# DeltaNet in a hybrid decoder step: the 16x16 diagonal blocks of each tile's triangular inverse are solved on VectorE and carried there and back by DMA, and the work of neighbouring tiles is put in another order

## The chip, the core and the metric

The kernel runs on one core of a Trainium2 chip. The core has a matrix engine (TensorE, PE), a vector engine (VectorE, DVE), a scalar engine (ScalarE, ACT), a general engine (GpSimd, POOL) and SyncE (SP), which issues DMAs. They run side by side and wait for each other through semaphores. The time is that of the device for one launch, in microseconds (us), as the median of several runs; lower is better.

## The reference

One layer of a decoder that mixes tokens with a gated DeltaNet and a forgetting attention, and channels with a mixture of 64 experts. The change is in the DeltaNet of the prompt: 512 tokens, 8 heads of 64 dimensions, chunks of 64 tokens. Cut to it:

```
lmat = beta[..., :, None] * jnp.einsum('nbhik,nbhjk->nbhij', k, k) * dec_strict
rhs = beta[..., None] * jnp.concatenate([v, gam[..., None] * k], axis=-1)
sol = lax.linalg.triangular_solve(lmat, rhs, left_side=True, lower=True, unit_diagonal=True)
w1, w2 = sol[..., :dv], sol[..., dv:]
aqk = jnp.einsum('nbhik,nbhjk->nbhij', q, k) * dec_incl
...
def step(s, xs):
    u = w1c - jnp.einsum('bhck,bhkv->bhcv', w2c, s)
    o = jnp.einsum('bhck,bhkv->bhcv', qgc, s) + jnp.einsum('bhij,bhjv->bhiv', aqkc, u)
    s = glc[..., None, None] * s + jnp.einsum('bhck,bhcv->bhkv', kdc, u)
    return s, o
```

The triangular system is unit lower triangular, 64x64 for each chunk and head.

## The kernel before

The kernel is one program in phases, with a barrier of all engines between them; every wait and every order of instructions is written by hand. `arena` is all of SBUF, `bank` the eight PSUM banks. The phase here does the DeltaNet of the prompt in four tiles of 128 tokens (`t`, PT = 4), each of two chunks (`ch`), for 8 heads in two halves of four (`hb`). In one tile:

- Transposes (L1355) of keys, scaled keys, queries and scaled queries; the decay rows (L1360); the key and query products (L1364). ScalarE copies and takes the exponentials (L1534, L1537). VectorE makes from them `LT`, the masked and decayed key products, whose 64x64 blocks are to be inverted, and `dec` (L1479, L1485, L1486).
- The inverse by doubling, in six levels (`NL`): blocks of 1, 2, 4, 8, 16 and 32 are joined. Level 0 is a mask and a subtraction. In each later level a mask picks the off-diagonal blocks (`Lm`, L1468), TensorE multiplies twice (L1386 `Lm` by the transposed inverse, copied by ScalarE at L1554; L1396 by the inverse `Um`), VectorE subtracts (L1504) and TensorE transposes the new inverse (L1404, copied at L1557).
- The w products (L1410, L1411), and then the two chunks one after the other: state read (L1424), u on VectorE (L1512), output and state products (L1430 to L1432), new state (L1513, L1515). Then the output is copied and summed (L1518, L1519); the next tile's transposes wait for that.

Between these steps TensorE does parts of two other products of the layer that nothing here needs, the gate logits and the later modulation. They are the 80 later pieces (`PIECES`): "gate" pieces (L1194), "raw" pieces (L1189) and short "rows" pieces (L1180). `later_pieces(pe, place, count)` puts the next `count` of them at a place, and `later_out(act, place)` is ScalarE's copy of what they made. They read 2 MB slabs of weights into two slots. SyncE issues the loads of the slabs (`send_later(j)`, L220), each as soon as the last piece that read the same slot is done; its queue takes everything in order. Of the 80 pieces, 12 are in the phase before.

GpSimd runs the recurrence of the sample tokens at the same time (L1604 to L1636), four passes over 128x2048 elements, all in SBUF: L1618, six sums at L1614, three small operations, L1623, L1624, L1625, L1626, six sums. Because of it the kernel keeps some of VectorE's second operands in PSUM (`by_psum`, and the masks in banks 4 and 5).

Of the kernel before, what the change touches and what calls it, by code (L numbers as in the profile page):

```python
# [107 lines left out]
def build(nc, A, O):  # L108
# [39 lines left out]
    def const(*dims, p=P):  # L148
        nonlocal c
        v = at(c, *dims, p=p)  # L150
        c += int(np.prod(dims))
        return v
    ident, causneg, cumU, ones = const(P), const(P), const(P), const(P)
    chunk1, chunkU, decneg = const(P), const(P), const(P)
    strictL, strictU = const(P), const(P)
    lvl = const(6, P)
# [10 lines left out]
    nF = const(TOK, p=H)  # L167
    cT, w24 = const(KD, QUAD), const(KD, 24)
    nm, rsum, rinv = const(PT * H), const(PT * H), const(PT * H)
    lfp = const(DB * NPG, H)  # L170
# [91 lines left out]
    with nc.Block() as block:  # L262
        @block.gpsimd
        def _(pool):
# [26 lines left out]
            for l in range(6):  # L291
                b = 2 << l
                n = P // b
                fill(lvl[:, l, :].rearrange("p (n r) -> p n r", n=n), (1.0, 0.0), (ge, 0, 1, [[-b, n], [0, b]]),
                     (ge, b // 2 - 1, -1, [[b, n], [0, b]]), (ge, -(b // 2), 0, [[0, n], [1, b]]))
# [940 lines left out]
    with nc.Block() as block:  # L1236
# [77 lines left out]
    trT = at(X0 + 9472, 4, CW, P)  # L1314

    rows_of = [at(T1 + 6912, 4, W), at(T1 + 9472, 4, W)]
    kd_of = [at(T2, W), at(T1 + 8960, W)]
    LT, dec, Lm0, Tm, Um, P1 = (at(T2 + 512 + 1024 * i, H, P) for i in range(6))
    Lm_of = [Lm0, at(X0 + 4096, H, P)]
# [7 lines left out]
    r_done, tr_mm, tr_sb, kk_mm, gr_mm, dec_sub, dec_exp, lt_done = (Tick(nc, n) for n in (  # L1327
        "scaled_rows", "gdn_T_in_psum", "gdn_T_copied", "kk_product", "decay_rows", "decay_diffs", "decay_matrix", "LT_done"))
    lm_done, p1_mm, p1_sb, q_mm, u_sb, t_mm, t_sb = (Tick(nc, n) for n in (
        "level_masked", "LT_product", "LT_product_copied", "TLT_product", "inverse_updated", "inverse_T", "inverse_T_copied"))  # L1330
# [3 lines left out]
    t_act, masks_in = Tick(nc, "later_inverse_T_copied"), Tick(nc, "level_masks_in_psum")  # L1334
    S_kept, ro = at(T1 + 4096, CW, HD), at(T1 + 12216, NT, H)
    CONTENDED, mask0_in = 2, Tick(nc, "first_mask_in_psum")
    by_psum = bank[5][:, P:P + 3 * H].rearrange("p (i h) -> p i h", h=H)
    NL = 6
    KK_BANK = (2, 3, 4, 5)

    with nc.Block() as block:
        @block.tensor
        def _(pe):
            for t in range(PT):
                rows4, kd = rows_of[t % 2], kd_of[t % 2]
                nw2T = rows4[:, 1].rearrange("p (c n) -> p c n", c=CW)

                later_pieces(pe, (t, "state before"), 1)
                pe.wait_ge(r_done.sem, 3 * t + 2)
                if t:  # L1350
                    pe.wait_ge(o_sb.sem, t)
                srcs = [qkv_tm[:, t, W:2 * W], rows4[:, 0], qkv_tm[:, t, 0:W], rows4[:, 1]]
                for i, s in enumerate(srcs):
                    for cc in range(CW):
                        mm = nc.tensor.transpose(bank[i][:, cc * P:(cc + 1) * P], s[:, cc * P:(cc + 1) * P], ident)  # L1355
# [3 lines left out]
                for h in range(H):  # L1359
                    nc.tensor.matmul(bank[h // 4][:, (h % 4) * P:(h % 4 + 1) * P], E8[:, h, :], GT[:, t * P:(t + 1) * P], start=True, stop=True)  # L1360
                pe.wait_ge(tr_sb.sem, 4 * t + 4)
                for h in range(H):
                    r = slice(HD * (h % 2), HD * (h % 2) + HD)
# [3 lines left out]
                later_pieces(pe, (t, "decay"), 3)  # L1367
                later_pieces(pe, (t, "masks"), 2)
                for l in range(NL):
                    Lm = Lm_of[l % 2]  # L1370
                    for hb in range(2):
                        n = 2 * (NL * t + l) + hb
                        heads = range(4 * hb, 4 * hb + 4)
                        pe.wait_ge(lm_done.sem, n + 1)
                        col = lambda h: slice((h % 4) * P, (h % 4 + 1) * P)
                        if l == 0:
                            for h in heads:
                                mm = nc.tensor.transpose(bank[hb][:, col(h)], Lm[:, h, :], ident)
                            p1_mm.inc(mm)
                        else:  # L1380
                            if l == 1:
                                pe.wait_ge(t_sb.sem, 2 * t + hb + 1)
                            else:
                                pe.wait_ge(t_act.sem, 2 * ((NL - 2) * t + l - 2) + hb + 1)
                            for h in heads:
                                mm = nc.tensor.matmul(bank[hb][:, col(h)], Lm[:, h, :], Tm[:, h, :], start=True, stop=True)  # L1386
                            p1_mm.inc(mm)
                    if l == 0:
                        later_pieces(pe, (t, 0), 1)
                        continue  # L1390
                    for hb in range(2):
                        heads = range(4 * hb, 4 * hb + 4)
                        k = 2 * ((NL - 1) * t + l - 1) + hb
                        pe.wait_ge(p1_sb.sem, k + 1)
                        for h in heads:
                            mm = nc.tensor.matmul(bank[2 + hb][:, col(h)], P1[:, h, :], Um[:, h, :], start=True, stop=True)  # L1396
                        q_mm.inc(mm)
                    later_pieces(pe, (t, l), 1)
                    if l < NL - 1:
                        for hb in range(2):  # L1400
                            heads = range(4 * hb, 4 * hb + 4)
                            pe.wait_ge(u_sb.sem, 2 * (NL * t + l) + hb + 1)
                            for h in heads:
                                mm = nc.tensor.transpose(bank[hb][:, col(h)], Um[:, h, :], ident)  # L1404
                            t_mm.inc(mm)
# [1438 lines left out]
```

## Time and profile before

| | |
|---|---|
| median of 3 runs | 1685.38 us (1684.54 to 1686.4) |
| the profiled execution | 1679.23 us, its span 1677.1 us |
| mean granted TensorE clock | 0.961 of full speed |
| busy | TensorE 92%, VectorE 36%, ScalarE 19%, GpSimd 19% |
| the DeltaNet phase | from 476 to 781 us |

The profiled execution is one run of the program on the chip. Times in its views are from the start of the span. Busy time is the sum of the instructions of an engine; matmuls overlap, so a row that merges several says from when to when they ran. "[3.15 <-PE bank L1396]" behind a row is the idle time of its engine ahead of it and what ended it.

### The profile page before, as it was taken

What the parts mean: (1) busy time and instruction counts of PE and PEld (TensorE: products, weight loads), DVE (VectorE), ACT (ScalarE), POOL (GpSimd) and SP (SyncE); (2) the same over time, 40 slices, a digit from 0 to 9 for tenths busy, and PEclk for the clock granted to TensorE, in tenths of its full rate; (3) what the DMA queues carried; (4) which work ended last, traced back from release to release, by engine and by line L of the source; (5) the groups of instructions that cost most, each with busy time, mean ns of one, the idle gap of its engine ahead of it and who ended that gap; (6) DMA issues with size and microseconds to landing.
All of it is one profiled execution on the core that took longest, in us unless ns stands there. A gap on an engine that the chain in (4) does not pass through costs nothing. (4 is left out here: it accounts for less than half of the span.)

```text
span 1677.1 us, 21451 instructions
## 1 busy us (share of the span) xinstructions
PE 1537.2 (92%) x8238; PEld 898.8 (54%) x8238; DVE 610.4 (36%) x1261; ACT 320.8 (19%) x704; POOL 313.8 (19%) x341
## 2 busy tenths in 40 slices
PE   5999999999989899999999688999989989898966
PEld 3876666664568787777755433343334433333322
DVE  2002543342374536354558743331111111111128
ACT  1002222333232223231201200111101111111121
POOL 6000000000039994000001421111111111111100
PEclk8999999999999999999999888999999999999978
DMA  9312110123162126114740157999999999999765
GB/s 340 120 51 84 52 52 0 51 63 101 64 182 100 68 71 187 68 57 145 264 158 26 42 203 314 388 415 411 415 421 391 413 412 403 408 378 422 285 253 241
DMA packets 104481, 357.16 MB, mean 213 GB/s; under 512 B 27731, under 2 KB 28883, under 8 KB 78259
## 3 DMA queue, kind: packets, MB, share of 16 engines
q1 hardware_dynamic: 79414, 302.11, 46.5%
q0 software_dynamic: 15520, 39.17, 6.2%
q10 hardware_dynamic: 9446, 14.51, 2.4%
q8 instruction: 66, 1.08, 0.3%
q14 instruction: 35, 0.29, 0.1%
HBM read 330.70 MB, written 37.62 MB: 220 GB/s over the span
## 5 line engine op out<-in xcount | busy, mean ns | idle before, releaser
L1985 PE MATMUL bank<-arena 128*32 128x512 f32 (+2 forms) x1536 | 334.0, 611 | 23.8 <-DMA arena<-in_w_up 22.9
L1985 PEld LDWEIGHTS bank<-arena 128*32 128x32 f32 (+2 forms) x1536 | 119.9, 138 | 205.6 <-issue 202.9
L1993 PE MATMUL bank<-arena 128*32 128x512 f32 (+2 forms) x768 | 168.6, 598 | 0.7 <-DVE arena L2740 0.7
L1972 POOL DMA_INDIRECT expert_rows<-arena x46 | 46.5, 1010 | 486.2 <-PE bank L1978 419.7
L2734 DVE TENSOR_TENSOR arena<-arena,bank 128x256 f32<-128x256 f32 x46 | 19.4, 421 | 323.7 <-ACT arena L2388 323.7
L1194 PE MATMUL bank<-arena 128*128 128x272 f32 x512 | 128.0, 398 | 1.2 <-ACT arena L1231 1.0
L429 PE MATMUL bank<-arena 128*128 128x272 f32 x480 | 113.9, 400 | 2.8 <-PEq L132 1.8
L1993 PEld LDWEIGHTS bank<-arena 128*32 128x32 f32 (+2 forms) x768 | 55.0, 134 | 110.3 <-issue 109.4
L1194 PEld LDWEIGHTS bank<-arena 128*128 128x128 f32 x512 | 93.3, 190 | 22.8 <-issue 2.9
L429 PEld LDWEIGHTS bank<-arena 128*128 128x128 f32 x480 | 93.0, 194 | 23.3 <-issue 2.7
L658 PE MATMUL bank<-arena 128*128 128x272 f32 x384 | 103.6, 416 | 0.0
L446 PE MATMUL bank<-arena 128*128 128x512 f32 (+3 forms) x304 | 88.1, 449 | 2.6 <-ACT arena L2330 2.2
L2388 ACT ACTIVATE arena<-bank 128x256 f32<-128x256 f32 x46 | 17.6, 383 | 347.4 <-PE bank L1985 347.4
L658 PEld LDWEIGHTS bank<-arena 128*128 128x128 f32 x384 | 73.8, 202 | 17.2 <-issue 3.4
L2746 DVE COPY arena<-bank 128x512 f32<-128x512 f32 x46 | 31.8, 691 | 126.9 <-PE bank L1993 126.9
L446 PEld LDWEIGHTS bank<-arena 128*128 128x128 f32 (+1 forms) x304 | 46.9, 193 | 42.5 <-issue 38.7
L1600 POOL TENSOR_TENSOR arena<-arena 128x512 f32<-128x512 f32 x5 | 7.7, 1535 | 314.8 <-POOLq L1236 314.5
L2450 POOL DMA_INDIRECT expert_lists<-arena x34 | 35.1, 1032 | 140.5 <-DVE arena L2576 131.3
L1978 PE MATMUL bank<-arena 128*128 128x128 f32 x368 | 49.5, 279 | 7.6 <-DMA arena<-h_rows,arena 7.6
L2394 ACT COPY arena<-bank 128x512 f32<-128x512 f32 x46 | 27.0, 587 | 152.5 <-PE bank L1993 152.5
L1968 POOL DMA_INDIRECT arena<-h_rows,arena x46 | 47.2, 1027 | 39.7 <-DVE arena L1912 20.0
L1504 DVE TENSOR_TENSOR arena<-arena,bank 128x512 f32<-128x512 f32 x40 | 27.5, 687 | 67.2 <-PE bank L1396 66.9
(468 smaller groups left out, 2108.5 us busy)
## 6 DMA issues: line engine op xcount, KB each, us to landing
arena<-in_w_gate SPq DMA_DIRECT2D x64, 1024.0 KB
arena<-in_w_up SPq DMA_DIRECT2D x64, 1024.0 KB
arena<-in_w_down SPq DMA_DIRECT2D x64, 1024.0 KB, 17.6
arena<-in_w_ada SPq DMA_DIRECT2D x12, 2048.0 KB, 8.8
arena<-in_w_in SPq DMA_DIRECT2D x11, 2048.0 KB, 9.9
arena<-expert_rows SPq DMA_DIRECT2D x8, 2048.0 KB, 25.6
gate_logits<-arena ACTq DMA_DIRECT2D x16, 272.0 KB, 3.8
arena<-gate_logits SPq DMA_DIRECT2D x8, 544.0 KB, 5.1
```

The source lines that it names most:

```text
L429: mm = nc.tensor.matmul(pair[i][:, 0:HALF], w[:, k, m * P:(m + 1) * P], rhs[:, k, i * HALF:(i + 1) * HALF], start=k == 0, stop=k == kt - 1)
L446: mm = nc.tensor.matmul(out, lhs[:, k, t * P:t * P + n], w[:, k, cols], start=k == 0, stop=k == kt - 1)
L658: mm = nc.tensor.matmul(out[:, 0:HALF], w[:, k, (m % 4) * P:(m % 4 + 1) * P], hT[:, k, half * HALF:(half + 1) * HALF], start=k == 0, stop= ...
L1194: mm = nc.tensor.matmul(out[:, 0:HALF], w[:, k, m * P:(m + 1) * P], hT[:, k, half * HALF:(half + 1) * HALF], start=k == 0, stop=k == KD - 1)
L1504: done(u_sb, nc.vector.tensor_tensor(Um[:, hs, :], Um[:, hs, :], bank[2 + hb].ap().rearrange("p (h n) -> p h n", h=4), ALU.subtract))
L1968: return nc.gpsimd.indirect_dma_start(out=into, out_offset=None, in_=h2_d, in_offset=bass.IndirectOffsetOnAxis(ap=rows, axis=0), bounds_ch ...
L1972: return nc.gpsimd.indirect_dma_start(out=y_d, out_offset=bass.IndirectOffsetOnAxis(ap=rows, axis=0), in_=of, in_offset=None, bounds_check ...
L1978: mm = nc.tensor.transpose(bank[half][:, k * P:(k + 1) * P], of[:, kk * P:(kk + 1) * P], ident)
L1985: mm = nc.tensor.matmul(out[rows].rearrange("p (a n) -> p a n", a=2), x[:, k, rows], gate_up_slot(n)[:, :, k, :], start=k == 0, stop=k == ...
L1993: mm = nc.tensor.matmul(out[rows, :], h[:, k, rows], down_slot(n)[:, k, 512 * half:512 * half + 512], start=k == 0, stop=k == 1)
L2450: scat.inc(nc.gpsimd.indirect_dma_start(out=list_rows, out_offset=bass.IndirectOffsetOnAxis(ap=adi[:, t, k:k + 1], axis=0), in_=tokval[:, ...
L2746: nc.vector.tensor_copy(Yb[u % RY][:, 512:D], bank[6][:, :]).then_inc(y_v.sem, 1)
```

## The change

- VectorE no longer masks and subtracts at levels 0 to 3. For each tile SyncE stores the eight 16x16 diagonal blocks of `LT` per head to DRAM (`key_blocks`) in 8 transfers of 16 partitions, and loads them back with 2 transfers of 64 partitions so that a partition holds one block of one head (`n16`, on two halves of the partitions). VectorE inverts each block there by 15 steps of two operations (`block_inverses`, each half of the partitions eight of the sixteen columns). SyncE stores the result in 2 transfers, waits for it, and puts it on the diagonal of `Um` in 8 transfers of 16 partitions.
- Only the levels that join blocks of 16 and of 32 are left on TensorE (`NL` = 2). ScalarE copies their off-diagonal blocks out of `LT` in 6 copies; `Lm` is zeroed once, `Um` once a tile. No masks are made or kept.
- The order of a tile: levels, then the transposes, decay and key products of the next tile (`keys_and_decays(t + 1)`), then the w products and both chunks of this tile, then the next tile's `block_inverses` on VectorE. `dec` and the scaled queries get a second buffer each, so that both tiles can be under way.
- The later pieces move: 15 behind the first tile's key products and 2 ahead of its levels, then 4 ahead of each tile's levels, 4 behind each tile's key products, and 5 or 6 at the other places.

The core of the diff:

```diff
@@ VectorE
-            def level_mask(t, l):
...
+            def block_inverses(t):
+
+                dve.wait_ge(n16_in.sem, 32 * (t + 1))
+                for j in range(15):
+                    n = 15 - j
+                    row = (i16 if j == 0 else x16)[:, :, j:j + 1].to_broadcast([P, 8, n])
+                    step(nc.vector.tensor_tensor(p16[:, :, 0:n], row, n16[:, j:j + 1, j + 1:16].to_broadcast([P, 8, n]), ALU.mult))
+                    ins = nc.vector.tensor_tensor(x16[:, :, j + 1:16], (i16 if j == 0 else x16)[:, :, j + 1:16], p16[:, :, 0:n], ALU.subtract)
+                    done(x16_done, ins) if j == 14 else step(ins)
...
+                inverse_level(t, 1)
+                if t + 1 < PT:
+                    keys_and_decays(t + 1)
                 dve.wait_ge(w_mm.sem, t + 1)
...
+                states(t, 0)
+                if t + 1 < PT:
+                    step(nc.vector.memset(Um, 0.0))
+                states(t, 1)
...
                 if t < PT - 1:
+                    block_inverses(t + 1)
@@ TensorE
+            def levels(t):
+                later_pieces(pe, (t, "inverse back"), 4 if t else 2)
+                pe.wait_ge(um_in.sem, 16 * NB * (t + 1))
+                if t:
+                    pe.wait_ge(o_sb.sem, t)
...
+            later_pieces(pe, "state before", 2)
+            keys_and_decays(0)
+            for t in range(PT):
+                levels(t)
+                if t + 1 < PT:
+                    keys_and_decays(t + 1)
+                weighted_rows(t)
+                states(t, 0)
+                later_pieces(pe, (t, "state between"), 1 if t + 1 < PT else 2)
+                states(t, 1)
@@ ScalarE
+                for b in range(4):
+                    rows, cols = slice(32 * b, 32 * b + 16), slice(32 * b + 16, 32 * b + 32)
+                    ach.inc(nc.scalar.copy(Lm_of[0][rows, :, cols], LT[rows, :, cols]))
@@ SyncE
-            for j in range(3, len(LATER)):
-                send_later(j)
+            def store_key_blocks(t):
+                sp.wait_ge(lt_done.sem, t + 1)
+                for a in range(NB):
+                    b16 = slice(16 * a, 16 * a + 16)
+                    n16_out.inc(sp.dma_start(n16_d[a].rearrange("h j i -> j h i"), LT[b16, :, b16]), 16)
+
+            def load_key_blocks(t):
+                sp.wait_ge(n16_out.sem, 16 * NB * (t + 1))
+                for g in range(2):
+                    n16_in.inc(sp.dma_start(n16[64 * g:64 * g + 64], n16_d.rearrange("a h j i -> (a h) j i")), 16)
+
+            def move_block_inverses(t):
+                sp.wait_ge(x16_done.sem, t + 1)
+                for g in range(2):
+                    x16_out.inc(sp.dma_start(x16_d[:, :, g].rearrange("a h r i -> (a h) r i"), x16[64 * g:64 * g + 64]), 16)
+                sp.wait_ge(x16_out.sem, 32 * (t + 1))
+                for a in range(NB):
+                    b16 = slice(16 * a, 16 * a + 16)
+                    um_in.inc(sp.dma_start(Um[b16, :, b16], x16_d[a].rearrange("h g r i -> (g r) h i")), 16)
+
+            send_later(3)
+            store_key_blocks(0)
+            send_later(4)
+            load_key_blocks(0)
+            send_later(5)
+            move_block_inverses(0)
+            send_later(6)
+            store_key_blocks(1)
```

SyncE before the change, behind the loads for the sample recurrence: the nine slabs (in_w_in and in_w_ada) and then the new state.

```order
L1581 DMA arena<-sample_gates 64x8
L220 DMA arena<-in_w_in 128x8x512
L220 DMA arena<-in_w_ada 128x8x512 x2
L220 DMA arena<-in_w_in 128x8x512
L220 DMA arena<-in_w_ada 128x8x512 x2
L220 DMA arena<-in_w_in 128x8x512
L220 DMA arena<-in_w_ada 128x8x512 x2
L1592 DMA out_ssm_prompt<-arena 64x4x64 x2
```

SyncE of the change at the same place, up to the second tile's stores (the slabs are L223 there).

```order
L223 DMA arena<-in_w_in 128x8x512
L1645 DMA key_blocks<-arena 16x8x16 x8
L223 DMA arena<-in_w_ada 128x8x512
L1650 DMA arena<-key_blocks 64x256 x2
L223 DMA arena<-in_w_ada 128x8x512
L1655 DMA key_block_inverses<-arena 64x128 x2
L1659 DMA arena<-key_block_inverses 16x8x16 x8
L223 DMA arena<-in_w_in 128x8x512
L1645 DMA key_blocks<-arena 16x8x16 x8
L1650 DMA arena<-key_blocks 64x256 x2
```

Slabs and block transfers take turns in one queue now: the first slab stands ahead of the first tile's stores, the second ahead of its loads, the third ahead of its inverses.

TensorE before the change, from the first tile's key products (L1364) into its third level (L1194, L1189 and L1180 are the later pieces).

```order
L1364 MATMUL bank<-arena 128x256 x8
L1194 MATMUL bank<-arena 128x272 x12
L1180 MATMUL bank<-arena 32x128 x4
L1194 MATMUL bank<-arena 128x272 x4
L1378 MATMUL bank<-arena 128x128 x8
L1194 MATMUL bank<-arena 128x272 x4
L1386 MATMUL bank<-arena 128x128 x8
L1396 MATMUL bank<-arena 128x128 x8
L1194 MATMUL bank<-arena 128x272 x4
L1404 MATMUL bank<-arena 128x128 x8
L1386 MATMUL bank<-arena 128x128 x8
L1396 MATMUL bank<-arena 128x128 x8
```

TensorE of the change from the same key products (L1372) to the last pieces ahead of the levels; L1192, L1187 and L1178 are the later pieces, L1384 is the transpose of the loaded inverse blocks.

```order
L1372 MATMUL bank<-arena 128x256 x8
L1192 MATMUL bank<-arena 128x272 x8
L1178 MATMUL bank<-arena 32x128 x4
L1192 MATMUL bank<-arena 128x272 x24
L1187 MATMUL bank<-arena 32x512 x8
L1192 MATMUL bank<-arena 128x272 x16
L1178 MATMUL bank<-arena 32x128 x4
L1192 MATMUL bank<-arena 128x272 x8
L1384 MATMUL bank<-arena 128x128 x8
L1392 MATMUL bank<-arena 128x128 x8
L1397 MATMUL bank<-arena 128x128 x8
```

Seventeen pieces now stand between the first tile's key products and its first level, where six did.

## Rows read from the trace of the kernel before

**Rows 1.** Windows, whole phase: stretch, its length, then busy (instructions) by engine, clock, DMA.
```profile
476.00:781.00 305.00, 286.43 (x2250) 233.24 (x2250) 143.77 (x219) 80.44 (x184) 151.71 (x102) 0.99 0.29 94
```

**Rows 2.** Timeline of TensorE, one level of the second tile: start, length, instruction.
```profile
592.92 2.02 PE L1386 MATMUL bank<-arena 128*128 128x128 f32 x16 [0.33 <-ACT arena L1557]
594.78 2.00 PE L1396 MATMUL bank<-arena 128*128 128x128 f32 x16
...
598.45 1.04 PE L1404 MATMUL bank<-arena 128*128 128x128 f32 x8
599.82 2.02 PE L1386 MATMUL bank<-arena 128*128 128x128 f32 x16 [0.33 <-ACT arena L1557]
```

**Rows 3.** Timeline of TensorE, other steps of a tile, and the last.
```profile
535.11 0.43 PE L1410 MATMUL bank<-arena 128*128 128x64 f32 x2
...
540.93 2.10 PE L1194 MATMUL bank<-arena 128*128 128x272 f32 x8
...
554.30 0.43 PE L1180 MATMUL bank<-arena 128*32 128x128 f32 x8
556.68 1.94 PE L1355 MATMUL bank<-arena 128*128 128x128 f32 x16 [1.96 <-DVE arena L1519]
...
562.36 2.00 PE L1364 MATMUL bank<-arena 64*128 64x256 f32 x16
...
778.44 2.27 PE L452 MATMUL bank<-arena 128*128 128x128 f32 x18
```

**Rows 4.** Timeline of VectorE, first tile, first and last operation of the decay.
```profile
487.30 1.43 DVE L1479 TENSOR_TENSOR bank<-bank,arena 128x512 f32<-128x512 f32 x2 [2.84 <-PE bank L1364]
...
493.52 0.42 DVE L1486 TENSOR_TENSOR arena<-bank,arena 128x256 f32<-128x256 f32 x1
```

**Rows 5.** Groups by form, VectorE, whole span: busy us, mean ns, idle before.
```profile
L2553 DVE TENSOR_TENSOR arena<-arena 128x8 f32<-128x8 f32 x5 | 0.9, 172 | 0.2
...
L251 DVE TENSOR_TENSOR arena<-arena 128x128 f32<-128x128 f32 x2 | 0.6, 293 | 0.1
```

**Rows 6.** SyncE's timeline, and DMA issues 470 to 800: KB each, us to landing.
```profile
476.12 8.30 SPq L1573 DMA_DIRECT2D sample_rows<-arena  x24
...
later_modulation<-arena ACTq DMA_DIRECT2D x32, 16.0 KB, 1.7
...
arena<-in_x_sample SPq DMA_DIRECT2D x1, 128.0 KB, 14.0
...
arena<-sample_gates SPq DMA_DIRECT2D x2, 2.0 KB, 2.9
```

**Rows 7.** Timelines of VectorE and of GpSimd, both inputs in SBUF.
```profile
476.23 8.23 DVE L1453 TENSOR_TENSOR arena<-arena 128x512 f32<-128x512 f32 x5
...
498.31 3.60 DVE L1499 TENSOR_TENSOR arena<-arena 128x512 f32<-128x512 f32 x1
...
551.37 0.42 DVE L1513 TENSOR_TENSOR arena<-arena 128x256 f32<-128x256 f32 x1
...
497.73 3.64 POOL L1618 TENSOR_TENSOR arena<-arena 128x2048 f32<-128x2048 f32 x1
...
546.88 5.49 POOL L1624 TENSOR_SCALAR arena<-arena 128x2048 f32<-128x2048 f32 x1
```

**Rows 8.** The first slab of the phase on SyncE, and such slabs' landing.
```profile
493.44 0.59 SPq L220 DMA_DIRECT2D arena<-in_w_in  x1
...
arena<-in_w_in SPq DMA_DIRECT2D x3, 2048.0 KB, 8.8
```

**Rows 9.** Timeline of GpSimd, parts of the first pass, and the last sums.
```profile
518.17 4.54 POOL L1625 TENSOR_TENSOR arena<-arena 128x2048 f32<-128x2048 f32 x1
...
526.50 5.77 POOL L1614 TENSOR_TENSOR arena<-arena 128x1024 f32<-128x1024 f32 x6
...
630.32 6.16 POOL L1614 TENSOR_TENSOR arena<-arena 128x1024 f32<-128x1024 f32 x6
```

**Rows 10.** Windows, the start of the next phase.
```profile
798.00:805.00 7.00, 6.46 (x15) 4.94 (x16) 0.00 (x0) 1.34 (x2) 2.74 (x16) 0.53 0.97 317
```

More of the change, by code:

```diff
@@ L1366, in _ @@
                 kk_mm.inc(mm)
-                later_pieces(pe, (t, "decay"), 3)
-                later_pieces(pe, (t, "masks"), 2)
+                later_pieces(pe, (t, "decay"), 15 if t == 0 else 4)
+            def levels(t):
[3 more added lines that the diff above has]
+                    pe.wait_ge(o_sb.sem, t)
+                for hb in range(2):
+                    for h in range(4 * hb, 4 * hb + 4):
+                        mm = nc.tensor.transpose(bank[hb][:, col(h)], Um[:, h, :], ident)
+                    t_mm.inc(mm)
@@ L1369, in _ @@
                 for l in range(NL):
-                    Lm = Lm_of[l % 2]
+                    k = 2 * (NL * t + l)
+                    pe.wait_ge(lm_done.sem, t + 1)
                     for hb in range(2):
[L1372 to L1387, printed above, removed]
@@ new lines, in take_P1 @@
+            def take_P1(t, l):
+                k = 2 * (NL * t + l)
+                for hb in range(2):
+                    act.wait_ge(p1_mm.sem, k + hb + 1)
+                    p1_sb.inc(nc.scalar.copy(P1[:, 4 * hb:4 * hb + 4, :], bank[hb].ap().rearrange("p (h n) -> p h n", h=4)))
+            later_out(act, "state before")
+            keys_and_decays(0)
+            for t in range(PT):
+                if 0 < t < PT - 1:
+                    act.wait_ge(o_sb.sem, t)
+                    scales_to_psum(t + 1)
+                later_out(act, (t, "inverse back"))
+                take_T(t, 0)
+                take_P1(t, 0)
+                later_out(act, (t, "level"))
+                take_T(t, 1)
+                take_P1(t, 1)
+                if t + 1 < PT:
+                    keys_and_decays(t + 1)
@@ L1561, in _ @@
                 w2_sb.inc(nc.scalar.mul(nw2T, bank[5].ap().rearrange("p (c n) -> p c n", c=CW), -1.0))
[L1562 to L1565 removed]
+                for place in ((t, "w"), (t, "state", 0), (t, "state between"), (t, "state", 1)):
+                    later_out(act, place)
             for tick in (mod_out, *gate_out):
@@ L1596, in _ @@
             step = chained(pool, gch)
+            for g in range(2):
+                half = i16[64 * g:64 * g + 64]
+                step(pool.memset(half, 0.0))
+                i16_made.inc(pool.affine_select(out=half, in_=half, compare_op=ALU.not_equal, fill=1.0, base=8 * g,
+                                                pattern=[[1, 8], [-1, 16]], channel_multiplier=0))
+            pool.wait_ge(i16_made.sem, 2)
             for t in range(NT):
```

281 lines of the change are left out of this document (149 added, 132 removed).

## The prediction

> **What bounds the kernel now.** The page of the profile gives TensorE 92% of the span, so I read where it is not busy, and what the DeltaNet stage holds. The stretch from 476 to 781 us is that stage: 305 us, of which TensorE is busy 286.43 [rows 1]. Little of it is waiting, so the stage costs what its matmuls cost. One level of the inverse takes from 592.92 to 599.82, 6.90 us: two products of 2.02 and 2.00, a later piece of 2, a transpose of 1.04 [rows 2]. The rest of a tile: the transposes, a piece, the decay rows and the key products from 556.68 to 564.36; the w products from 535.11 to 540.93; both chunks with their pieces from 540.93 to 554.30 [rows 3].
>
> **What goes away.** Of the 15 blocks of eight matmuls that a tile's inverse has on TensorE (5 transposes, 10 products) the order keeps 6 (2 transposes, 4 products). That is 3 x 1.04 + 6 x 2.01 = 15.2 us a tile, 61 us in all [rows 2]. The 80 later pieces stay, only at other places. So 61 us is the most that can be won, and it is won only where TensorE finds something else than a wait.
>
> **A tile after the change.** Levels: a transpose first, then 6.90, then the two products of the last level without a piece or transpose, and about 0.6 for the copies between: 12.5 us. Next tile's keys: 7.7 plus four pieces at about 2.0: 15.8, which covers the 6.3 us that VectorE and ScalarE need for the decay (from the matmuls' end at 487.2 to 493.5 plus 0.4) [rows 4]. The w products 5.8, the chunks 13.4 [rows 3]. In sum 47.5 for tiles 0 to 2. The last has no next keys and one piece of 0.4 more: 32.1. All four: 174.6.
>
> **The new chain.** Before its levels can start a tile needs: VectorE's 30 small operations, two stores, a wait for them, eight loads.
> - VectorE alone: 8 values a partition take 172 ns and 128 take 293 [rows 5], so about 160 ns plus 1.04 ns a value. Thirty operations over 8n values (n from 15 to 1, twice each: 1,920 values) are 4.8 + 2.0, and 30 gaps of 0.04: 8.0 us.
> - The way back through DRAM: SyncE issued 24 small transfers of 4 partitions in 8.30 us, 0.35 each; these have 16, and I choose 0.5. Small stores landed in 1.7, small loads in 2.9 [rows 6]. Two stores to their landing 2.3; seven issues of loads 3.5; the last load with its semaphore 3.0: about 9 us. Bounds: 0.35 an issue, with landings of 1.3 and 2.2, 6.6; twice my issues and twice the landing of the loads, 15.
> - VectorE's own end of a tile (state, two copies, sum), after which the transposes could start at 556.68, 2.3 behind the last product [rows 3].
> Four pieces lie beside it on TensorE, 7.3 us. Without anything else a tile waits 2.3 + 8.0 + 9.0 - 7.3 = 12 us.
>
> **GpSimd in the way.** The sample recurrence runs on GpSimd from 497.7 to 636.5 [rows 7, 9]. Where both inputs of a VectorE operation are in SBUF it is held until the GpSimd operation ends, and then the two alternate: five operations of 512 values took 8.23 us, 1.65 each, and one at 498.31 took 3.60 although it needs 0.69; it ended with L1618, which ran from 497.73 for 3.64 [rows 7]. All 30 new operations have both inputs in SBUF. One exception shows: at 551.37 such an operation took its plain 0.42 while the TENSOR_SCALAR of L1624 ran from 546.88 to 552.37 [rows 7]. The Trainium skill, page "SBUF — State Buffer", section "Who interferes with whom", says that a VectorE instruction with two SBUF inputs contends with a GpSimd instruction that reads SBUF, under an exclusive lock. The trace agrees for tensor-tensor operations and not for L1624, which reads SBUF too. I go by the rows: L1624 is a free window of 5.45 us in each pass of some 34 us.
>
> Tile 0. Key products end at 488, their blocks are masked 6.8 later, 494.7. The eight stores queue behind the gate slab that SyncE issued at 493.44, which takes 8.8 to land: 502.2; a 128 KB load behind two slabs took 14.0 to land, so a queue keeps its order [rows 6, 8]. SyncE then issues the next slab as soon as piece 19 is done, about 501.4, and the loads of the key blocks queue behind it: 510.5. VectorE waits for L1623 until 512.7; in L1624's window some 20 operations fit (5.8 us); the last ten wait for L1625 from 518.17 (4.54), L1626 (as L1618, 3.64), six operations of 5.77, and L1618 [rows 7, 9]. They end at 536. With 9 to move them the levels begin at 545. TensorE meanwhile has 17 pieces, 29 us: it ends them at 524 (it waits for the slab too) and then stands for 21.
> Tile 1. The levels of tile 0 end the chunks at 545 + 47.5 = 592.5, VectorE is free at 595. The six sums at 526.50 come again two passes later, at 596 [rows 9]: these (5.8), L1618 (3.7), six more (5.8), three small ones (1.2) and L1623 (3.7) hold seventeen operations, the other thirteen take 2.7 in L1624's window: 23 us instead of 8, and the tile waits 27 instead of 12.
> Tiles 2 and 3 come after 640, when GpSimd is done: 12 each.
>
> **The clock.** After sparse work the granted clock fell to 1.2 GHz: from 798 to 805 it was 0.53 although TensorE was busy 6.46 of 7 us, then 1.00 again [rows 10]. Each of the four waits is longer than the pauses ahead of that. Per wait (1 - 0.53) x 7 = 3.3 us, 13.2 in all. Low end nothing.
>
> **The sum.** 69 to the first levels (476 to 545) + 174.6 + (2.3 + 23 + 9) + 2 x (2.3 + 8 + 9) + a tail of 2.6 from the last product, at 778.4 before [rows 3] + 13.2 = 332.3 us, against 305: 27.3 slower. The profiled execution took 1679.23, so 1706.5 in its terms; the median of the runs is 6.15 above it: **1712 us**. Its own range is 1697 to 1727: 11 either way for where VectorE meets L1624, 10 for the transfers, added as independent.
>
> Costed at nothing: the masks that GpSimd no longer makes at the kernel's start, where TensorE waits for weights; three memsets in VectorE before the late scaled rows, beside TensorE's first pieces and transposes (else 3); ScalarE's six block copies: the copies of the later pieces queue behind them, so TensorE's fourth piece of tile 0 waits, but inside its wait for the slab (else 5). SyncE's slabs are behind the block transfers; from the sums each lands 5 us or more before its piece. If one did not, it is up to 8.8.
>
> **Rivals.**
> - *Faster: the small operations are not held.* They are 0.17 to 0.29 us, and might slip between GpSimd's operations; the held rows were all of 256 to 512 values. Then tile 0 starts at 527.5 and tile 1 waits 12: 332.3 - 17.5 - 15 = 299.8, 5 faster; with the cheap transfers (6.6) 15 faster: 1670 to 1680. It decides as soon as the holds cost less than 5 us together. Against it: five operations of one engine and five of the other took strict turns at 476, which needs an order and no size [rows 7]. Chance 0.24.
> - *The same.* Both blocks meet L1624 at its start, with 12 each: 13 and 11 less, 3 slower: 1688. Chance 0.09.
> - *L1624 holds them too*, as the rule of the Trainium skill on the page named above has it. Worked from rows: 30 operations against 30 of GpSimd's are a pass and a half, 54 us for tile 0 (31 more); tile 1 then meets GpSimd's last 13 us (6 less): 1738. Chance 0.07.
> - *The transfers cost 15 a tile*: 24 more, 1736. Chance 0.06.
> The forecast has the other 0.54.
>
> **Numbers.** 0.2%, 3.4 us, is about what a measurement of this kernel can tell from no change. Faster 0.25, same 0.07, slower 0.68. The range leaves out the two dear rivals (0.13) and the edge of the fast one in which the clock holds too (0.05): 1669 to 1728.
>
> **What would show it.** TensorE's busy time in the stage down by 61 us plus what a lower clock adds; L1493 and L1494 with means of 0.2 us in tiles 2 and 3 and 0.7 to 1 in tiles 0 and 1; TensorE waiting for the loaded inverse blocks about 20, 27, 12 and 12 us; the stage ending near 808. The forecast is wrong if tile 0's small operations take 8 us, if the loads land in half the time, or if the clock stays at 2.4 GHz in the waits.

## The result, and the profile after

Nine runs of each kernel gave a median of 1692.54 us (1689.45 to 1695.86) after the change and 1684.54 us (1670.84 to 1688.30) before it: ratio 1.0052, 95% interval 1.0028 to 1.0076. The change costs 8 us, where 27 were forecast; 1692.54 lies below the forecast's own range (1697 to 1727) and inside the wide one (1669 to 1728).

The profiled execution of the changed kernel took 1695.86. Windows of its trace: the DeltaNet stage, which answers to [rows 1], and two of TensorE's waits; columns as there.
```profile
478.56:806.99 328.43, 228.54 (x1771) 182.80 (x1771) 156.86 (x259) 63.35 (x157) 150.81 (x106) 0.85 0.30 91
528.00:556.00 28.00, 0.59 (x3) 0.16 (x1) 21.36 (x24) 0.39 (x1) 26.43 (x20) 0.55 0.03 5
609.00:648.00 39.00, 0.80 (x5) 0.51 (x4) 28.47 (x32) 0.00 (x0) 31.98 (x23) 0.55 0.20 37
```
TensorE does 58 us less in the stage than in [rows 1], at a granted clock of 0.85 for 0.99, and the stage is still 23 us longer than that one. Where the time went, in TensorE's waits (us, times, longest):
```profile
PE bank L1384 <- DMA arena<-key_block_inverses: 86.3, 4, 38.2
```
That is 86.3 us in four waits, the longest 38.2. Three of them in the timeline:
```profile
556.09 0.69 PE L1384 MATMUL bank<-arena 128*128 128x128 f32 x2 [27.50 <-DMA arena<-key_block_inverses]
647.49 1.97 PE L1384 MATMUL bank<-arena 128*128 128x128 f32 x8 [38.20 <-DMA arena<-key_block_inverses]
710.43 1.97 PE L1384 MATMUL bank<-arena 128*128 128x128 f32 x8 [10.60 <-DMA arena<-key_block_inverses]
712.31 3.36 PE L1392 MATMUL bank<-arena 128*128 128x128 f32 x16
```
The fourth wait is 9.98. They were forecast at 21, 27, 12 and 12. The last row, behind a wait, is the same work as the 2.02 us of [rows 2]; it takes 3.36, at a granted clock of 0.50 from 711 to 715 (1.2 of 2.4 GHz).

What they wait for is in VectorE's groups, the two lines of the new solve in tile 0 (window 514.9 to 548.7) and in tile 2 (695.2 to 703.1); columns are count, then busy us and the mean of one in ns:
```profile
L1493 DVE TENSOR_TENSOR arena<-arena 128x120 f32<-128x120 f32 (+14 forms) x15 | 17.4, 1158 | 18.2 <-DMA arena<-key_blocks 17.7
L1494 DVE TENSOR_TENSOR arena<-arena 128x120 f32<-128x120 f32 (+14 forms) x15 | 15.3, 1019 | 0.5
...
L1493 DVE TENSOR_TENSOR arena<-arena 128x120 f32<-128x120 f32 (+14 forms) x15 | 3.4, 226 | 0.5
L1494 DVE TENSOR_TENSOR arena<-arena 128x120 f32<-128x120 f32 (+14 forms) x15 | 3.4, 225 | 0.5
```
The same 30 operations take 33.6 us in tile 0 (515.05 to 548.70) and 31.5 in tile 1 (603.74 to 635.23), while GpSimd runs its recurrence, and 7.8 in tiles 2 and 3. The timeline of VectorE at the start of tile 0's solve, and below it that of GpSimd (POOL), show how:
```profile
515.05 3.13 DVE L1493 TENSOR_TENSOR arena<-arena 128x120 f32<-128x120 f32 x1 [17.74 <-DMA arena<-key_blocks]
518.22 0.28 DVE L1494 TENSOR_TENSOR arena<-arena 128x120 f32<-128x120 f32 x1
...
519.76 0.26 DVE L1493 TENSOR_TENSOR arena<-arena 128x96 f32<-128x96 f32 x1
520.06 4.45 DVE L1494 TENSOR_TENSOR arena<-arena 128x96 f32<-128x96 f32 x1
524.54 3.67 DVE L1493 TENSOR_TENSOR arena<-arena 128x88 f32<-128x88 f32 x1
528.25 2.38 DVE L1494 TENSOR_TENSOR arena<-arena 128x88 f32<-128x88 f32 x1
```
```profile
514.34 5.44 POOL L1723 TENSOR_SCALAR arena<-arena 128x2048 f32<-128x2048 f32 x1
519.87 4.53 POOL L1724 TENSOR_TENSOR arena<-arena 128x2048 f32<-128x2048 f32 x1
524.47 3.64 POOL L1725 TENSOR_TENSOR arena<-arena 128x2048 f32<-128x2048 f32 x1
528.19 5.73 POOL L1713 TENSOR_TENSOR arena<-arena 128x1024 f32<-128x1024 f32 x6
```
Read the ends: 520.06 + 4.45 is 524.51, just behind the end of L1724 (524.40) and the start of the next GpSimd operation (524.47); 524.54 + 3.67 is 528.21, just behind the start of the one after it (528.19). Where GpSimd's operations follow each other without a pause, one small operation gets in behind each of them, whatever its size. L1723, of which the prediction made a free window of 5.45 us (it is L1624 of before), is free only at its end: the operation at 515.05 is done at 518.18, 3.84 us into it, and then six go through at 0.26 to 0.28.

### The profile page after: what moved, and what is told of

It reads as the page before. It is cut to its first block and busy times, and to the rows that moved or that the text cites. A ratio compares the mean times of both kernels' runs of the same rounds, so it can differ in the third digit from the quotient of the medians.

```text
span 1694.1 us, 20463 instructions
## 1 busy us (share of the span) xinstructions
PE 1479.2 (87%) x7758; PEld 847.2 (50%) x7758; DVE 622.5 (37%) x1300; ACT 303.6 (18%) x676; POOL 301.7 (18%) x321
## 5 line engine op out<-in xcount | busy, mean ns | idle before, releaser
L1192 PE MATMUL bank<-arena 128*128 128x272 f32 x512 | 128.9, 403 | 7.1 <-ACT arena L1229 6.9
L1192 PEld LDWEIGHTS bank<-arena 128*128 128x128 f32 x512 | 95.2, 192 | 33.8 <-ACT arena L1229 8.4
L1384 PE MATMUL bank<-arena 128*128 128x128 f32 x32 | 7.9, 427 | 86.3 <-DMA arena<-key_block_inverses 86.3
L2077 PE MATMUL bank<-arena 128*128 128x128 f32 x368 | 49.5, 279 | 7.2 <-DMA arena<-h_rows,arena 7.2
L1493 DVE TENSOR_TENSOR arena<-arena 128x120 f32<-128x120 f32 (+14 forms) x60 | 48.5, 809 | 19.8 <-DMA arena<-key_blocks 17.7
L2067 POOL DMA_INDIRECT arena<-h_rows,arena x46 | 47.3, 1027 | 39.7 <-DVE arena L2011 20.2
```

Source lines behind the costliest of these rows:

```text
L1192: mm = nc.tensor.matmul(out[:, 0:HALF], w[:, k, m * P:(m + 1) * P], hT[:, k, half * HALF:(half + 1) * HALF], start=k == 0, stop=k == KD - 1)
L1493: step(nc.vector.tensor_tensor(p16[:, :, 0:n], row, n16[:, j:j + 1, j + 1:16].to_broadcast([P, 8, n]), ALU.mult))
L2067: return nc.gpsimd.indirect_dma_start(out=into, out_offset=None, in_=h2_d, in_offset=bass.IndirectOffsetOnAxis(ap=rows, axis=0), bounds_ch ...
L2077: mm = nc.tensor.transpose(bank[half][:, k * P:(k + 1) * P], of[:, kk * P:(kk + 1) * P], ident)
```

## The experiments

In this section the stage is measured from the start of its first transposes to the start of the first transposes behind it, which all kernels have (309.1 us in the first profile of before, 331.9 in that of after). Times are medians in us; ratios are to the kernel before in the same rounds, with 95% intervals. Medians of different rows come from different rounds and are not compared with each other.

| kernel | stage | solves, tiles 0 and 1 | median | ratio |
|---|---|---|---|---|
| before (six profiles) | 309.1, 319.5, 321.7, 321.6, 322.0, 321.7 | | | |
| before against itself | 321.7 | | 1694.29 | 0.9995 (0.9963 to 1.0027) |
| after (three profiles) | 331.9, 331.9, 331.1 | 33, 32 | 1702.34 | 1.0057 (1.0035 to 1.0079) |
| after, operands in PSUM | 285.7 | 7.8, 7.7 | 1658.28 | 0.9810 (0.9758 to 0.9863) |
| after, products alone in PSUM | 308.1 | 26.5, 19.3 | 1679.26 | 0.9926 (0.9899 to 0.9952) |
| after, no recurrence | 285.4 | 7.8, 7.8 | 1658.40 | 0.9832 (0.9780 to 0.9884) |
| before, no recurrence | 307.7 | | 1679.34 | 0.9927 (0.9901 to 0.9954) |
| after, kept warm | 321.0 | 31.7, 29.8 | 1699.52 | 1.004 (1.001 to 1.007) |
| PSUM, kept warm | 283.2 | 7.8, 7.8 | 1651.32 | 0.978 (0.9747 to 0.9813) |
| the same, branch weights later | 276.8 | 7.7, 7.7 | 1647.34 | 0.9738 (0.9705 to 0.9771) |
| PSUM, stage lengthened | 321.1 | 7.7, 7.7 | 1693.97 | 0.9988 (0.9951 to 1.0024) |

### The operands of the solve in PSUM

```diff
+    n16_ps = bank[2][:, 0:256].rearrange("p (j i) -> p j i", j=16)
+    p16_ps = bank[3][:, 0:128].rearrange("p (r i) -> p r i", r=8)
...
+                step(nc.vector.tensor_copy(n16_ps, n16))
...
-                    step(nc.vector.tensor_tensor(p16[:, :, 0:n], row, n16[:, j:j + 1, j + 1:16].to_broadcast([P, 8, n]), ALU.mult))
-                    ins = nc.vector.tensor_tensor(x16[:, :, j + 1:16], (i16 if j == 0 else x16)[:, :, j + 1:16], p16[:, :, 0:n], ALU.subtract)
+                    step(nc.vector.tensor_tensor(p16_ps[:, :, 0:n], row, n16_ps[:, j:j + 1, j + 1:16].to_broadcast([P, 8, n]), ALU.mult))
+                    ins = nc.vector.tensor_tensor(x16[:, :, j + 1:16], (i16 if j == 0 else x16)[:, :, j + 1:16], p16_ps[:, :, 0:n], ALU.subtract)
```


> The changed kernel with the solve's factors copied to a PSUM bank (one more VectorE copy a tile) and its products written to PSUM, so that no small VectorE operation has two SBUF sources. Theory H (in tiles 0 and 1 the solve is stretched from 7.8 to 33.6 and 31.5 us because GpSimd's recurrence holds VectorE's operations of two SBUF sources): each solve takes 8 to 10 us, the waits for the loaded inverses fall to about 5, 15, 11 and 10 us, the stage to about 280 us and the time to 1640 to 1655, below both kernels. Theory D (the moves by DMA and the queue set the waits): the solve may shrink but the levels start no earlier, time 1685 to 1695. Theory Q (any VectorE operation is slow while GpSimd runs): solve stays above 25 us, no change of time.

The time fell as theory H had it, to 1658.28, though not quite to 1655. The copy of the factors takes 0.43 us a tile. The solve's multiplications in this kernel's trace, least, median and longest in ns:
```profile
L1496 DVE TENSOR_TENSOR bank<-arena,bank x60: 173/229/288, 515.3 to 715.5; 128x120 f32<-128x120 f32 x4, 128x112 f32<-128x112 f32 x4, 128x104 f32<-128x104 f32 x4, 128x96 f32<-128x96 f32 x4
```
Its TensorE's waits:
```profile
PE bank L1386 <- DMA arena<-key_block_inverses: 39.7, 4, 17.2
```
And the longest, in tile 2, in its timeline:
```profile
661.51 1.97 PE L1386 MATMUL bank<-arena 128*128 128x128 f32 x8 [17.23 <-DMA arena<-key_block_inverses]
```
None of the 60 is longer than 0.288 us (none of the 60 subtractions than 0.279), beside the same GpSimd operations. The solves of tiles 0 and 1 together are 50 us shorter and the stage 46. This version beats both kernels. The 17.2 us in tile 2 was not foreseen; the section on a load that met the third move is about it.

### Without the recurrence, after and before

```diff
-            for t in range(DS):
-                kt, qt = sx[:, t, 1, :], sx[:, t, 0, :]
...
-                sum_keys(so[:, t, :])
+            step(pool.memset(so, 0.0))
```


> The changed kernel without GpSimd's recurrence over the sample tokens (their output rows are filled with zeros instead), VectorE's operations as they are. Theory H: solves of tiles 0 and 1 take 8 us each, the first two waits fall by 25 and 23 us (less where another operand is late), the stage to about 280 us, time 1640 to 1655, the same as with the operands in PSUM. Theory D: waits and time stay within 5 us of the changed kernel.

> The kernel before without GpSimd's recurrence over the sample tokens (their output rows are filled with zeros). It is the fourth corner beside before, after, and after without the recurrence: it says what the change is worth where nothing holds VectorE. In the profiles of before the stage took 309.1 and 319.5 us from its first transpose to the first transpose behind it, with granted clocks of 0.99 and 0.97. Theory: before has only large VectorE operations in the contended tiles and most of their sources are PSUM banks, so it loses little to GpSimd: 0 to 10 us gained, time ratio to before 0.994 to 1.0, and the change alone would be worth 25 to 37 us. Rival: before loses as much as after does in those tiles (over 25 us gained), and then the hold explains the level of both kernels but not the difference.

These two kernels leave the recurrence out, so their sample outputs are not those of the layer; they are there for the times. Taking GpSimd's work away gives the changed kernel the same solves of 7.8 us as the operands in PSUM did. So the solve is slow because of GpSimd, and because of operands that both lie in SBUF. That the two stages agree as well (285.4 and 285.7) is in part chance. Without the recurrence GpSimd's stores and its 2 MB load are issued from 497 to 518 us; there the first solve begins 38.6 us after the stage's start (34.8 with the operands in PSUM), and the first move back takes 11.0 us. With the operands in PSUM it is the third move that is long, 13.6.

The kernel before gains 0.7% (12 us) without the recurrence, a little above what was expected. With nothing to hold VectorE the change makes the kernel faster, 0.9832 against 0.9927, some 16 us (give or take 10), less than the 25 to 37 that were expected. The holds cost the changed kernel 37 us (1.0052 less 0.9832, of 1684.5; give or take 10) and the one before 12: they turn the sign.

### The products alone in PSUM

The edit is that of the first experiment without the copy: the subtractions then read one operand in SBUF, the multiplications still two.

> The changed kernel with only the solve's products in PSUM: the 15 subtractions of a tile then have one SBUF source, the 15 multiplications still two. Theory H2 (an operation is held if it has two SBUF sources, and one gets in behind each of GpSimd's): the held operations halve, the solves of tiles 0 and 1 take 16 to 20 us in place of 33.6 and 31.5, the subtractions keep 170 to 290 ns, the time lies about half way, at a ratio of 0.99 to before. Rival H1 (an operation is held by any SBUF source, and PSUM for all of them is needed): solves stay at 30 us or more, ratio 1.005.

The subtractions (L1495) and the multiplications (L1494) in this trace, four tiles each:
```profile
L1495 DVE TENSOR_TENSOR arena<-arena,bank x60: 168/220/280, 510.8 to 732.9; 128x120 f32<-128x120 f32 x4, 128x112 f32<-128x112 f32 x4, 128x104 f32<-128x104 f32 x4, 128x96 f32<-128x96 f32 x4
...
L1494 DVE TENSOR_TENSOR bank<-arena x60: 174/266/4161, 508.6 to 732.7; 128x120 f32<-128x120 f32 x4, 128x112 f32<-128x112 f32 x4, 128x104 f32<-128x104 f32 x4, 128x96 f32<-128x96 f32 x4
```
With one source in SBUF no operation is held, with two up to 4.16 us: H2's condition holds. Its size does not quite: tile 0 took 26.5 us, not 16 to 20, of which the 15 multiplications are some 22; tile 1 took 19.3. The time came out half way, 0.9926. Rival H1, that one SBUF source is enough to be held, is refuted. The Trainium skill, page "SBUF — State Buffer", section "Who interferes with whom", says that a VectorE instruction with at most one SBUF input, outside its 2-port modes, which tensor-tensor operations do not have, does not contend with GpSimd, and one with two does where GpSimd reads SBUF. These two rows agree with it. The Trainium skill, same page, section "Summary: rules for kernel authors", says that of two such instructions the second to issue is blocked until the first finishes. GpSimd's TENSOR_TENSOR rows agree with that; L1723 does not, beside which a held operation was done after 3.84 of its 5.44 us.

### The clock in the waits

`keep_warm` gives TensorE products of the identity that nobody reads; they stand ahead of its wait for the loaded inverses.

```diff
+                if t:
+                    pe.wait_ge(o_sb.sem, t)
+                keep_warm(bank[0][:, 384:512], (110, 150, 38, 38)[t])
                 pe.wait_ge(um_in.sem, 16 * NB * (t + 1))
```


> The changed kernel with products of the identity that nobody reads (110, 150, 38, 38) put into TensorE's four waits for the loaded inverses. Theory C (the clock that falls during a wait costs 2.5 to 3 us at each of them behind it): granted clock of the stage up from 0.85 to 0.97 or more, stage and time 8 to 12 us shorter, ratio to before 0.998 to 1.001. Rival: the time follows the VectorE chain and the clock costs nothing there: within 3 us of the changed kernel, ratio 1.004 to 1.006.

> The changed kernel with all of the solve's extra operands in PSUM, and 6, 58, 36 and 36 idle products of the identity in what is left of the waits. Theory C: 6 to 10 us less than with the operands in PSUM alone, ratio to before 0.975 to 0.978. Rival: the same as with the operands alone, 0.981.

Windows from 478 to 803, first of the changed kernel:
```profile
478.00:803.00 325.00, 225.04 (x1726) 179.54 (x1727) 154.90 (x254) 63.60 (x157) 150.81 (x106) 0.85 0.30 91
```
and of the one kept warm:
```profile
478.00:803.00 325.00, 305.26 (x2468) 259.30 (x2468) 162.69 (x268) 65.44 (x160) 148.99 (x102) 0.98 0.33 102
```
The granted clock stayed up and the stage lost 10.9 us. Not all of this is the clock: the two held solves were 3.6 us shorter, having met GpSimd otherwise, tile 1's move back took 9.1 us in place of 12.3, and the first solve began 2.1 later. The clock is read from what TensorE does behind the four waits, from the first product of the levels to the next solve, or to the stage's end. Together these stretches took 184.2, 183.3 and 183.9 us in the three profiles of the changed kernel and 183.9 with the operands in PSUM, against 177.8 and 178.7 in the two kernels kept warm: 6.0 and 5.2 us less, 1.3 to 1.5 a wait.

The time shows less than that: 1.004 against 1.0052 and 1.0057, with intervals that overlap. On top of the PSUM operands the stage lost only 2.5 us, because in tile 1 the idle products outlasted the loads: the levels began 10.1 us behind the solve, where they began 7.5 behind it without them. The ratio went from 0.981 to 0.978, again within the intervals. So the clock's price is shown in the stage and not in the time.

### A load that met the third move

```diff
+            pool.wait_ge(um_in.sem, 16 * NB * 3)
             branch_in[1].inc(pool.dma_start(wbb, A["w_branch_b"][0].rearrange("(k p) n -> p k n", p=P)), 16)
```


> The kernel with operands in PSUM and warm waits, with GpSimd's load of the branch weights (2 MB) held back until the third tile's inverses are in. Theory W (the move back of that tile took 13.4 us instead of 7.4 because its loads shared the DMA engines with the branch weights and the slab): the third move takes 7.5 to 8.5, the stage 5 to 6 us less than 283.2, ratio about 0.975. Rival: the move stays at 13 us (something else slows it), no difference; or the weights then come late behind the stage and cost more than 5 us there.

The move back in tile 2, from the first store's issue to the levels, in the timeline without the edit:
```profile
644.98 1.10 SPq L1661 DMA_DIRECT2D key_block_inverses<-arena  x2
649.29 0.82 POOL L1744 DMA_DIRECT2D arena<-in_w_branch_b  x1
658.44 0.90 PE L1389 MATMUL bank<-arena 128*128 128x128 f32 x3 [9.08 <-DMA arena<-key_block_inverses]
```
and with it:
```profile
644.66 1.10 SPq L1661 DMA_DIRECT2D key_block_inverses<-arena  x2
652.12 1.09 PE L1389 MATMUL bank<-arena 128*128 128x128 f32 x8 [3.08 <-DMA arena<-key_block_inverses]
652.66 0.81 POOL L1745 DMA_DIRECT2D arena<-in_w_branch_b  x1 [2.41 <-DMA arena<-key_block_inverses]
```
The move took 7.5 us in place of 13.5 and the stage 6.4 less: theory W. Behind the stage the profiled execution was 2.0 us longer. This version has the lowest ratio of all, 0.9738, but its interval overlaps that of 0.978 without the edit: the gain of this one step is shown in the stage and not in the time.

The changed kernel has the same trouble in tile 1, where its move took 12.3 us (solve ended 635.23, levels 647.49) against 7.4 in the other tiles. GpSimd's stores of the sample states, issued at 638.01 and 640.47, lie in it; its window 640 to 643:
```profile
640.00:643.00 3.00, 0.00 (x0) 0.00 (x0) 0.00 (x0) 0.00 (x0) 2.77 (x3) 0.50 0.87 148
```
and its transfers issued from 630 to 650 (KB, us to landing):
```profile
out_ssm_sample<-arena POOLq DMA_DIRECT2D x2, 512.0 KB, 9.4
```
That these stores are the cause there was not tried by itself, but the other runs bear it out. In the two repeats of the changed kernel the stores are issued 2.8 us behind the solve's end, as here, and the move took 11.9 and 11.6 us. In the kernel kept warm they come 6.6 behind it: 9.1. In the kernels with the operands or the products in PSUM, and in the one without the recurrence, no store falls into tile 1's move: 7.4 to 7.5.

### Both kernels again, and a longer stage

> The kernel before, unchanged, profiled a second time. Its time is 1684.5 by the median. In the first profile the DeltaNet stage took 305.3 us and what came behind it 895.9 us, with stretches of low granted clock between 882 and 1013 us. If the 8.8 us that the rest of the program was longer there than in the profile of after are a chance of that one execution, the rest varies here (887 to 896 us) while the stage keeps 305 within 1 us. If the change really gives time back behind the stage, the rest is 896 here again.

> The changed kernel, unchanged, profiled a second time. The first profile had 328.4 us of stage and 887.1 us behind it. If the stage's loss is fixed by dependences, it is 328 again within 2 us, with the four waits for the loaded inverses at 27, 38, 11 and 10 us. If the gap between the loss in the stage (23 us) and the loss in the medians (8 us) is chance in one profile, stage or rest move here by several us; if the rest gives it back, it is 887 again.

> The kernel before against itself, on the chip and in the rounds of the others: ratio 1.000 within 0.3%. Its profile is the third of the stage: near 309 us as in the first, or near 319 as in the second, with a granted clock in the contended tiles to match. If the first was a fast exception, this one has 314 us or more.

> The changed kernel, unchanged, against before in the same rounds. The first comparison gave 1.0052 (1.0028 to 1.0076), 8 us; 1.003 to 1.008 is expected again, a stage of 332 us within 1, waits of 27, 38, 11 and 10 us. If the difference of the medians were to reach the 23 us of the first two profiles, the ratio would be 1.013.

Before against itself came out at 0.9995 and the change at 1.0057, as the first time. The stage of the changed kernel is the same in three profiles within 0.8 us. That of the kernel before was 309.1 in the profile that the prediction used and 319.5 and 321.7 in the next two, so I took three more.

> The kernel before, a fourth profile. If the stage of 309.1 us in the first profile was an exception, it has 316 us or more here, with held L1499 operations of 2 to 3.5 us in the second tile; if the stage has two levels that change from execution to execution, 309 or 320.

> The kernel before, a fifth profile, with the same question: 309 or 320 us of stage. If the time of an execution follows its stage, executions under 1685 have 309 and those over 1690 have 320.

> The kernel before, a sixth profile, with the same question: 309 or 320 us of stage.

321.6, 322.0 and 321.7, in executions of 1684.9, 1688.3 and 1687.7 us: the first profile was the exception, by 10 to 13 us. The timeline of the fourth shows two places where its 12.5 us go. By the second tile's transposes it is 2.9 us behind the first profile (80.1 us from the stage's start, 77.2 in the first), and 1.6 of these are there when the first tile's last state update (L1513, both inputs in SBUF) begins. In the first profile this is the operation at 551.37 of [rows 7], with its plain 0.42. In the fourth it began behind the start of L1625 and was held to its end:
```profile
552.19 4.33 DVE L1513 TENSOR_TENSOR arena<-arena 128x256 f32<-128x256 f32 x1
```
```profile
551.73 4.51 POOL L1625 TENSOR_TENSOR arena<-arena 128x2048 f32<-128x2048 f32 x1
```
It took 4.29 to 4.35 in all five later profiles. TensorE then waited 3.2 us for the transposes (1.96 in the first), and the granted clock from 560 to 565 was 0.53, where the first profile has 1.00; by its key products the fourth is 5.8 us behind. The other 6.7 come between its first level and its w products, with the second tile's sums of the identity and a masked block (L1499, both inputs in SBUF). In the first profile:
```profile
574.03 0.90 DVE L1499 TENSOR_TENSOR arena<-arena 128x512 f32<-128x512 f32 x1
575.69 0.91 DVE L1499 TENSOR_TENSOR arena<-arena 128x512 f32<-128x512 f32 x1
```
and in the fourth:
```profile
579.04 2.25 DVE L1499 TENSOR_TENSOR arena<-arena 128x512 f32<-128x512 f32 x1
582.05 3.37 DVE L1499 TENSOR_TENSOR arena<-arena 128x512 f32<-128x512 f32 x1
585.45 0.69 DVE L1501 TENSOR_TENSOR arena<-arena,bank 128x512 f32<-128x512 f32 x1
586.29 2.05 PE L1386 MATMUL bank<-arena 128*128 128x128 f32 x8 [2.99 <-DVE arena L1501]
```
In the first they fell beside the last, short sums of GpSimd's L1614. In the fourth they met L1623 and L1624, TensorE waited for them, and its granted clock over the 77 us from 555.7 was 0.89, where the first profile has 0.98 from 556.5 on. Without the recurrence L1513 takes 0.42 and L1499 0.69, and the stage of before 307.7. So in five of six profiles the kernel before pays some 12 us for held operations and the clock behind them, and the profile before the prediction was of the one that did not. Why the first tile was 1.6 us faster in that one stays open; its granted clock from 500 to 510 was 1.00, where the five have 0.83.

The rest of the program went the other way. A stretch of routing (from L2073 to L1978 of before) took 130.6 us in the first profile of before and 138.0, 138.2, 124.7, 124.9 and 124.7 in the others, and 125.4, 138.1 and 130.9 in those of after: three levels, whichever the kernel. In the first two profiles that took 5 us off the difference of 23 in the stage; their spans were 17 us apart, the medians 8.

> The changed kernel with the solve's operands in PSUM (ratio 0.981 to before, stage 285.7 us) and 160 more identity products behind the last chunk, which lengthen the DeltaNet stage by about 20 us at a full clock and touch nothing else. Theory P (what the stage takes is passed on in full): time and span 18 to 21 us above the version without them, ratio 0.992 to 0.993, and then the 6 us by which the rest was shorter in the profiles of after than of before are chance. Rival G (part is given back, since weights go on loading meanwhile): the rest of the program gets 3 to 8 us shorter, ratio 0.987 to 0.990.

I had taken the 160 products at about half of what they take: nine are 2.27 us in the last row of [rows 3], 0.25 each, and the stage grew by 35.4 us, 0.22 each. The ratio rose by 0.0178 (30 us, give or take 11), the profiled span by 39.7. So most of what the stage takes, if not all, is passed on; that 3 to 8 us come back is neither shown nor excluded.

## Why the prediction was off

The direction and the mechanism were right: VectorE's small operations held by GpSimd in tiles 0 and 1, TensorE waiting in each tile for the blocks, TensorE's busy time down by 58 us, where 61 less what a lower clock adds were forecast. The size was off by 19 us, and the step that failed is the last of **The sum**, "= 332.3 us, against 305: 27.3 slower": not the 332 but the 305. The stage of after, by the same bounds, came out at 328.4. The 305 was read in an execution in which three operations of the kernel before that GpSimd holds elsewhere fell into gaps; in the other five its stage is 10 to 13 us longer. The prediction had seen that this execution was 6.15 us below the median, and added these to the result as if they lay outside the stage. 27.3 less the 3.9 of the sum and less 12.5 for the base (the median of the six, 321.6, less 309.1) is 10.9 us, where the two timed comparisons have 8 and 9.6 (0.0057 of 1692). That the first profile's stage was short was neither in the bounds nor among the rivals, since every duration came from that one execution. The same chance gave the prediction its free window: the operation at 551.37, its only row for it, began 4.49 us into L1624, and in the five other profiles that operation comes after L1624 and is held.

Term by term, in the stage of after:
- **To the first levels**: 69 forecast, 77.5 measured. The key blocks came 36.5 us after the start (34.5), the solve took 33.6 (25.5), the move 7.4 (9). "L1624 is a free window" was wrong for its first 3.8 us: six operations went through, not some 20.
- **Tile 1**: 85.1 forecast with its wait and clock, 91.4 measured. The solve took 31.5 (23), the move 12.3 (9), the rest of the tile 47.7 (53.1).
- **Tiles 2 and 3**: 70.1 each forecast, 62.9 and 62.4 measured. Solve 7.8 (8.0), move 7.4 (9). In tile 2 levels, keys, w products and chunks up to the solve took 13.8, 15.4, 4.9 and 13.0, against 15.8, 15.8, 5.8 and 15.7 with the clock and VectorE's end. The chunks' step was read from 540.93, from a piece on that belongs to the w products.
- **Behind the last levels**: 38 forecast, 34.2 measured.
- **The clock**: 3.3 a wait forecast; 1.3 to 1.5 by the runs kept warm.
- 8.5 and 6.3 too little, 7.2, 7.7 and 3.8 too much: the sum is 3.9 high. That it came out so near is luck: the errors cancel.

Of the rivals, "not held" is refuted by the rows at 520.06. "L1624 holds them too" was right in what it said of the operation and wrong in its price: a held operation waits for an end, so small operations still pass in its last 1.6 us and beside GpSimd's short ones (from 543.54 on six in a row took 0.18 or 0.19). The transfers cost 7.4 us a tile, near the low bound of 6.6. SyncE's slabs were late for TensorE once, by 1.7 us at 514.73, where the prediction had it wait for a slab too. ScalarE's copies, costed at nothing with 5 in reserve, held TensorE for 5.4 us at 494.6, inside the time to the first levels.

## What to carry to other kernels

Before VectorE work is put beside GpSimd's, count its operations with two SBUF sources, not their elements: each costs up to what GpSimd's current operation still has to run, and one of the two operands in PSUM lifts this at the price of a copy (0.43 us here, for 25 us a tile). Where the stage to be changed has such operations itself, read it in several profiles of the kernel before: one can be 12 us off, and a window that one operation seems to show can be a chance of that execution. A chain of small transfers to DRAM and back cost 7.4 us here with nothing large beside it, and 9 to 13.6 when a large store or load had been issued from another queue.

## What the hardware showed that I had not expected

- GpSimd's TENSOR_SCALAR over 2,048 values (5.44 us) holds VectorE's two-source operations only at its start. In after L1723 starts at 514.34, and the operation that began at 515.05 was done at 518.18; that of the last pass starts at 617.34, and the operation that began at 617.64 was done at 621.17. They are done 3.84 and 3.83 us behind its start, and so are the four of the two repeats, whenever they began. Less their plain 0.22 to 0.28 us, that puts their start some 3.6 us into it (an estimate from these rows). GpSimd's TENSOR_TENSOR operations hold to the end. Only the start and the end of the held operations were seen, not why.
- GpSimd is delayed in turn by little: L1723 took 5.44 to 5.49 us with such operations waiting, L1624 of before up to 5.76.
- One stretch of the program, far from the change, took 124.7, 130.6 or 138 us in the same kernel; no run shows why.
- An operation of 8 values a partition waits as long as a large one: 3.65 us at 544.85 for 128x8.
